# Prompt attention of a two-layer decoder: units ordered head by head, with three score banks and three accumulators

## The chip, the cores and the metric

The kernel runs on one core of one Trainium2 chip. The metric is the device time of one execution in microseconds, the median of several runs.

In this document PE is TensorE (its weight loads have a row of their own, PEld), DVE is VectorE, ACT is ScalarE, POOL is GpSimd and SP is SyncE. PSUM has eight banks, here called bank 0 to bank 7.

## What is computed

Two layers run for a prompt of 512 positions and for eight samples of eight positions each. Each layer has a joint input projection, three mixers (retention, sparse attention, gated delta rule), and an output projection. The part that matters here is the sparse attention of the prompt: 8 query heads in 2 key groups, head width 64, and three branches whose outputs are added with a gate for each head and branch:

```python
o_cmp, imp = _nsa_compressed(q, pos, k_c, v_c)                  # branch 0: 31 compressed keys
o_sel = ... _nsa_sel_attend(q_rot, ...)                         # branch 1: selected blocks
o_win = ... _window_attend(q_rot, ...)                          # branch 2: window of 512
no = gate[:, :, 0] * o_cmp + gate[:, :, 1] * o_sel + gate[:, :, 2] * o_win
no = no.reshape(B, T, NSA_WIDTH) * jax.nn.silu(pr['nsa_g'].astype(jnp.float32))
```

With a prompt of 512 positions all eight blocks are selected and the window reaches back to the start, so branches 1 and 2 are both plain causal attention over all keys up to the query, and branch 0 has 31 keys. Each branch is a masked softmax over its keys times its values.

## The kernel before

A layer is a series of stages with a barrier between them: input projection, retention, delta rule, prompt attention (`prompt_attention`), sample attention, output projection. Both layers go through the same code.

The second stage of `prompt_attention` is where the change lies. It works on 192 **units**; a unit is one tile of 128 queries (`qt`, 0 to 3), one branch (`br`, 0 to 2) and one head (`h`, 0 to 7). A unit of branch 0 has 31 keys, one of branch 1 or 2 has (qt + 1) * 128 keys. The order is the list `units`: for each query tile all heads of branch 0, then all of branch 1, then all of branch 2.

Every engine walks that list with its own lag, and semaphores tie them together. For a unit u:

1. PE, in its iteration u, makes the scores and adds the mask (`scores`, lines 1441 and 1443) in the bank `sbank(u)`.
2. DVE takes the row maximum (line 1501) and scales it (line 1503) (`biggest`).
3. ACT makes the exponentials with their sum (line 1486) into `Pr`.
4. PE, in its iteration u + 2, transposes them 128 keys at a time (`turn`, line 1452).
5. DVE for even u, ACT for odd u, copies them to `PT` (`copy`, line 1431).
6. PE, in its iteration u + 3, multiplies with the values (`values`, line 1464) into the head's 64 columns of an accumulator bank.
7. After the eighth head of a branch, DVE merges (`merge`, lines 1511 to 1521): it inverts the sums, multiplies the gates in, scales the 512 columns of the accumulator, adds them to `NO` and, for the last branch of the tile, multiplies by the output gate.

So PE's iteration v is: scores of v, transposes of v - 2, values of v - 3. DVE's iteration v is: maximum of v, copy of v - 2 if that is even, and the merge after unit v - 3 if v - 3 was the last of its group of heads. Within an engine everything is in order: while DVE merges, no maximum and no copy is made.

Before the change `DEEP` is 4 (four score banks and four buffers of `Pr`), and the accumulators are two banks used in turn by the 12 groups of eight units.

Of the kernel before, what the change touches and what calls it, by code (L numbers as in the profile page):

```python
# [17 lines left out]
ALU = mybir.AluOpType  # L18
# [8 lines left out]
HD = 64  # L27
H4 = 4
NH, G, R = 8, 2, 4
WIN = 512  # L30
P = 128
# [143 lines left out]
def b_(ap, axis, shape):  # L175

    return ap.unsqueeze(axis).broadcast_to(shape)
# [1125 lines left out]
def prompt_attention(nc, A, O, l, scope, sb, stage, v, U):  # L1303


    bk, cb, ident, MIX = v['bk'], v['cb'], v['ident'], v['MIX']
# [13 lines left out]
    with stage(["dve_s", "act_s", "pe_s", "rows", "kv"]) as (block, (dve_s, act_s, pe_s, rows, kv)):  # L1320
# [5 lines left out]
        @block.sync  # L1326
        def _(e):
            for i in range(2):
                e.dma_start(PG[:, i, :, :], O['kv_prompt'][l, 0].rearrange("(t p r) a g d -> t p r (a g d)", p=P, r=PAIRS)[i, :, :, 0:256]).then_inc(rows, 16)
            e.dma_start(QRP[:, :, :, :].rearrange("p t i c -> p t (i c)"), A['q_rot'].rearrange("(t p) c -> p t c", p=P)).then_inc(rows, 16)  # L1330
            e.dma_start(A['new_kv'].rearrange("b t c -> (b t) c"), v['US'][0:64, NKV:NKV + CW]).then_inc(kv, 16)
            first_pages(e, A, l, v, 0)
            e.wait_ge(kv, 16)
            for i in range(2):
                e.dma_start(new_values(v['US'])[:, :, i, :], A['new_kv'].rearrange("b t c -> t b c")[:, :, 256 * (i + 1) + P:256 * (i + 2)]).then_inc(kv, 16)
            e.wait_ge(kv, 48)
# [64 lines left out]
                    dve.done(e, f"T{'kl'[g]}{t}", nc.vector.tensor_copy(KT[g * HD:(g + 1) * HD, g, :, t * P:(t + 1) * P], bk(2, 4)[g * HD:(g + 1) * HD, 0:2, :]))  # L1401

    early.close()
    DEEP = 4
    sbank = lambda u: bk((0, 1, 6, 7)[u % DEEP])
    Pr = sb(scope, "Pr", [P, DEEP, SEQ])
    PT = sb(scope, "PT", [P, 2, 4, P])
    mx = sb(scope, "mx", [P, DEEP, 2])
    SUM = sb(scope, "SUM", [P, 2, NH])
    fac = sb(scope, "fac", [P, NH])  # L1410
    T1 = sb(scope, "T1", [P, 512])
    NO = sb(scope, "NO", [P, 512])
    units = [(qt, br, h) for qt in range(4) for br in range(3) for h in range(NH)]
    NU = len(units)
    with stage(["score", "shift", "exped", "turned", "copied_dve", "copied_act", "used", "link_s", "merged"]) as \
            (block, (score, shift, exped, turned, copied_dve, copied_act, used, link_s, merged)):
        copied = [copied_dve, copied_act]

        def keys(u):
            qt, br, h = units[u]  # L1420
            return NCP if br == 0 else (qt + 1) * P

        def copy(e, u):

            n = keys(u)
            m, k = (n, 1) if n < P else (P, n // P)
            e.wait_ge(turned, u + 1)
            if u >= 2:
                e.wait_ge(used, u - 1)
            o, i = PT[0:m, u % 2, 0:k, :], bk(2 + u % 2, 4)[0:m, 0:k, :]  # L1430
            (nc.scalar.activation(o, i, ACT.Copy) if u % 2 else nc.vector.tensor_copy(o, i)).then_inc(copied[u % 2], 1)

        @block.tensor
        def _(e):
            def scores(u):
                qt, br, h = units[u]
                g, r, n = h // R, h % R, keys(u)
                if u >= DEEP:
                    e.wait_ge(exped, u - DEEP + 1)
                kt = KCG[:, g, 0:n] if br == 0 else KT[:, g, br - 1, 0:n]  # L1440
                nc.tensor.matmul(sbank(u)[:, 0:n], QT[:, min(br, 1), r, qt * P:(qt + 1) * P], kt, start=True, stop=False)  # L1441
                m = cb('cmask', 32)[:, qt, 0:n] if br == 0 else cb('causal')
                nc.tensor.matmul(sbank(u)[:, 0 if br == 0 else qt * P:n], cb('identb'), m, start=False, stop=True).then_inc(score, 1)  # L1443

            def turn(u):
                n = keys(u)
                e.wait_ge(exped, u + 1)
                if u >= 2:
                    e.wait_ge(copied[u % 2], u // 2)
                for j in range(-(-n // P)):  # L1450
                    m = min(P, n - j * P)
                    mm = nc.tensor.transpose(bk(2 + u % 2, 4)[0:m, j, :], Pr[:, u % DEEP, j * P:j * P + m], ident)  # L1452
                mm.then_inc(turned, 1)

            def values(u):
                qt, br, h = units[u]
                g, n, q = h // R, keys(u), u // NH
                e.wait_ge(copied[u % 2], u // 2 + 1)
                if h == 0 and q >= 2:
                    e.wait_ge(merged, q - 1)  # L1460
                for j in range(-(-n // P)):
                    m = min(P, n - j * P)
                    vv = VC[0:m, 0, g * HD:(g + 1) * HD] if br == 0 else U[j][:, NKV + P + 256 * br + g * HD:NKV + P + 256 * br + (g + 1) * HD]
                    mm = nc.tensor.matmul(bk(4 + q % 2)[:, h * HD:(h + 1) * HD], PT[0:m, u % 2, j, :], vv, start=(j == 0), stop=(j == -(-n // P) - 1))
                mm.then_inc(used, 1)

            for u in range(NU + 3):
                if u < NU:
                    scores(u)
                if 2 <= u < NU + 2:  # L1470
                    turn(u - 2)
                if u >= 3:
                    values(u - 3)

        @block.scalar
        def _(e):
            for u in range(NU + 2):
                if u >= 2 and u % 2:
                    copy(e, u - 2)
                if u < NU:  # L1480
                    qt, br, h = units[u]
                    n = keys(u)
                    e.wait_ge(shift, u + 1)
                    if u >= DEEP:
                        e.wait_ge(turned, u - DEEP + 1)
                    nc.scalar.activation(Pr[:, u % DEEP, 0:n], sbank(u)[:, 0:n], ACT.Exp, scale=SCALE, bias=mx[:, u % DEEP, 1:2],  # L1486
                                         accum_out=SUM[:, (u // NH) % 2, h:h + 1]).then_inc(exped, 1)

        @block.vector
        def _(e):  # L1490
            links = [0]

            def link(ins):
                links[0] += 1
                ins.then_inc(link_s, 1)
                e.wait_ge(link_s, links[0])

            def biggest(u):
                n = keys(u)
                e.wait_ge(score, u + 1)  # L1500
                link(nc.vector.tensor_reduce(mx[:, u % DEEP, 0:1], sbank(u)[:, 0:n], AX.X, ALU.max))  # L1501

                nc.vector.tensor_scalar(mx[:, u % DEEP, 1:2], mx[:, u % DEEP, 0:1], -1e20, -SCALE, ALU.max, ALU.mult).then_inc(shift, 1)  # L1503

            def merge(u):
                qt, br, h = units[u]
                q = u // NH
                hb = lambda ap: ap.rearrange("p (h c) -> p h c", c=HD)
                e.wait_ge(used, u + 1)
                e.wait_ge(exped, u + 1)  # L1510
                link(nc.vector.tensor_scalar(fac[:, :], SUM[:, q % 2, :], 1e-30, None, ALU.max))
                link(nc.vector.reciprocal(fac[:, :], fac[:, :]))
                link(nc.vector.tensor_tensor(fac[:, :], fac[:, :], U[qt][:, NGATE + br * NH:NGATE + (br + 1) * NH], ALU.mult))
                dst = NO if br == 0 else T1
                links[0] += 1
                nc.vector.tensor_tensor(hb(dst[:, :]), hb(bk(4 + q % 2)), b_(fac[:, :], 2, [P, NH, HD]), ALU.mult).then_inc(link_s, 1)
                e.wait_ge(link_s, links[0])
                if br:
                    link(nc.vector.tensor_tensor(NO[:, :], NO[:, :], T1[:, :], ALU.add))
                if br == 2:  # L1520
                    link(nc.vector.tensor_tensor(MIX[:, qt, 256:768], NO[:, :], U[qt][:, NG:NG + 512], ALU.mult))
                nc.vector.engine_nop().then_inc(merged, 1)

            for u in range(NU + 3):
                if u < NU:
                    biggest(u)
                if 2 <= u < NU + 2 and u % 2 == 0:
                    copy(e, u - 2)
                if u >= 3 and (u - 3) % NH == NH - 1:
                    merge(u - 3)  # L1530


# [641 lines left out]
```

## Time and profile before

| | |
|---|---|
| three runs | 2633.17, 2610.85, 2634.86 us; median 2633.17 |
| the profiled execution | 2642.13 us, its span 2640.5 us |
| busy over the span | PE 84%, PE's weight loads 63%, DVE 50%, ACT 28%, POOL 11% |
| mean granted clock of TensorE | 0.854 of full |

The span is the time from the first to the last instruction. "Granted clock" is what the throttle let TensorE have: 1.00 is 2.4 GHz, 0.50 is 1.2 GHz. A busy PE says only that some matmul was in flight, not that it ran at the full clock.

### The profile page before, as it was taken

The numbers are of one execution on the slowest core, as the hardware profiler recorded it, in microseconds if no ns is written. First come the engines' busy times: TensorE is split into PE (matmuls) and PEld (weight loads), VectorE is DVE, ScalarE is ACT, GpSimd is POOL, SyncE is SP. The second block draws the span as 40 slices with busy tenths as digits, with TensorE's granted clock in tenths as the row PEclk, the third lists the DMA queues.
The fourth block names the chain that finished last, engine by engine and source line by source line (L and its number), as shares of the span: only waits on it lengthen the run. The fifth ranks groups of instructions, "written<-read, shape, count | busy, mean of one in ns | idle before, by whom it ended". The sixth has DMA issues, their size and how long they took to land. (4 is left out here: it accounts for less than half of the span.)

```text
span 2640.5 us, 35927 instructions
## 1 busy us (share of the span) xinstructions
PE 2229.7 (84%) x12280; PEld 1657.8 (63%) x12280; DVE 1321.1 (50%) x3088; ACT 730.7 (28%) x1512; POOL 302.4 (11%) x516
## 2 busy tenths in 40 slices
PE   6989748738999999997889896586499999999977
PEld 3644448737767888886354444486376678888863
DVE  1252566534654666654213434765355556666532
ACT  2120002103434454440212101111044445444302
POOL 0000000000013433420000000000000234334100
PEclk9999769756879999996989997687567889999859
DMA  4443010020027886851035330100300368868420
GB/s 148 147 151 113 26 35 1 1 79 7 1 52 168 192 188 152 181 124 72 2 113 168 137 109 10 35 1 2 84 1 1 89 150 191 179 152 190 107 72 36
DMA packets 175947, 242.04 MB, mean 92 GB/s; under 512 B 50118, under 2 KB 132838, under 8 KB 175084
## 3 DMA queue, kind: packets, MB, share of 16 engines
q1 hardware_dynamic: 151180, 172.51, 24.5%
q0 software_dynamic: 24576, 67.14, 10.8%
q8 instruction: 100, 1.64, 0.3%
q14 instruction: 91, 0.75, 0.1%
HBM read 223.17 MB, written 24.97 MB: 94 GB/s over the span
## 5 line engine op out<-in xcount | busy, mean ns | idle before, releaser
L601 PE MATMUL bank<-W,hT 128*128 128x512 f32 (+3 forms) x1152 | 449.0, 544 | 30.6 <-DMA W<-in_w_in 21.5
L1282 POOL DMA_DIRECT2D SHARED<-in_cache_nsa_kv x256 | 151.5, 592 | 2048.7 <-issue 734.4
L601 PEld LDWEIGHTS bank<-W,hT 128*128 128x128 f32 x1152 | 219.0, 195 | 230.8 <-issue 184.5
L1225 PE MATMUL bank<-XT,W 128*128 128x256 f32 (+1 forms) x768 | 250.8, 462 | 0.0
L1214 ACT ACTIVATE XT<-bank 128x512 f32<-128x512 f32 x256 | 140.3, 593 | 132.6 <-PE bank L1207 132.5
L1282 POOL DMA_DIRECT2D PS<-in_cache_nsa_kv x256 | 150.7, 589 | 140.6 <-issue 128.2
L1225 PEld LDWEIGHTS bank<-XT,W 128*128 128x128 f32 x768 | 134.9, 190 | 49.7 <-issue 36.9
L1207 PE MATMUL bank<-CF,RP 128*128 128x128 f32 x1024 | 146.9, 290 | 7.6 <-DVE RP L1195 6.9
L1708 PE MATMUL bank<-QBD,PS 128*128 128x64 f32 x1024 | 141.9, 287 | 0.0
L1501 DVE TENSOR_REDUCE mx<-bank 128x1 f32<-128x31 f32 (+4 forms) x192 | 74.6, 389 | 132.5 <-PE bank L1443 131.1
L1708 PEld LDWEIGHTS bank<-QBD,PS 128*128 128x128 f32 x1024 | 139.7, 210 | 0.7
L1688 PEld LDWEIGHTS bank<-PB,PS 128*128 128x128 f32 x1024 | 132.7, 209 | 10.6 <-issue 6.7
L1688 PE MATMUL bank<-PB,PS 128*128 128x64 f32 x1024 | 135.1, 292 | 3.5 <-ACT PB L1854 3.5
L1207 PEld LDWEIGHTS bank<-CF,RP 128*128 128x128 f32 x1024 | 120.3, 151 | 18.9 <-DVE RP L1195 10.6
L1441 PE MATMUL bank<-KT,QT 128*128 128x128 f32 (+3 forms) x256 | 125.5, 580 | 0.0
L366 DVE COPY UP<-bank 128x512 f32<-128x512 f32 (+3 forms) x36 | 21.4, 604 | 199.9 <-PE bank L601 199.7
L2092 PE MATMUL bank<-Wo,mT 128*128 128x512 f32 x256 | 114.6, 611 | 5.9 <-DMA Wo<-in_w_out 5.9
L1486 ACT ACTIVATE Pr<-bank,mx 128x31 f32<-128x31 f32 (+4 forms) x192 | 85.6, 446 | 120.1 <-DVE mx L1503 119.1
L1195 DVE COPY RP<-SHARED 128x512 f32<-128x512 f32 x256 | 98.6, 426 | 24.9 <-DMA SHARED<-in_cache_nsa_kv 12.8
L368 ACT ACTIVATE UP<-bank 128x512 f32<-128x512 f32 (+3 forms) x36 | 18.7, 527 | 302.9 <-PE bank L601 302.8
L1452 PE MATMUL bank<-CF,Pr 128*128 128x128 f32 (+1 forms) x384 | 88.9, 317 | 14.8 <-ACT Pr L1486 14.8
L1858 ACT ACTIVATE PS<-bank 128x512 f32<-128x512 f32 x128 | 75.8, 593 | 89.2 <-PE bank L1695 88.3
(378 smaller groups left out, 3699.4 us busy)
## 6 DMA issues: line engine op xcount, KB each, us to landing
SHARED<-in_cache_nsa_kv SPq DMA_DIRECT2D x256, 128.0 KB, 6.1
SHARED<-in_cache_nsa_kv POOLq DMA_DIRECT2D x256, 128.0 KB, 5.3
PS<-in_cache_nsa_kv SPq DMA_DIRECT2D x256, 128.0 KB, 6.1
PS<-in_cache_nsa_kv POOLq DMA_DIRECT2D x256, 128.0 KB, 5.7
W<-in_w_in SPq DMA_DIRECT2D x48, 512.0 KB, 4.5
XS<-scratch_conv_p SPq DMA_DIRECT2D x24, 384.0 KB
PW<-in_state_nsa_win SPq DMA_DIRECT2D x16, 512.0 KB, 3.8
Wo<-in_w_out SPq DMA_DIRECT2D x4, 2048.0 KB, 11.8
```

The source lines that it names most:

```text
L601: return nc.tensor.matmul(bk((c * NTILE + t) % 8)[:, 0:b - a], hT[:, k, t * P:(t + 1) * P], W[:, k // 2, k % 2, 0:b - a], start=(k == 0), ...
L1195: dve.done(e, self.name("R", i), nc_(self.v).vector.tensor_copy(self.RP[:, i % self.RING, :, :, :].rearrange("p h r d -> p r h d"), self.P ...
L1207: mm = nc_(self.v).tensor.transpose(self.v['bk'](6 + i % 2, 4)[:, h, :], self.RP[:, i % self.RING, h, :, :].rearrange("p r d -> p (r d)"), ...
L1214: act.done(e, self.name("X", i), nc_(self.v).scalar.activation(self.columns()[:, :, :, i, :], self.v['bk'](6 + i % 2).rearrange("p (h s n) ...
L1225: mm = nc_(self.v).tensor.matmul(out, self.v['W1'][:, kv, s, :], seg[:, s], start=(s == 0), stop=(s == SEG // PAIRS - 1))
L1282: e.dma_start(where[side * HD:(side + 1) * HD, slot, :, :], A['cache_nsa_kv'][l, page].rearrange("(p r) a g d -> p r (a g d)", r=PAIRS)[:, ...
L1441: nc.tensor.matmul(sbank(u)[:, 0:n], QT[:, min(br, 1), r, qt * P:(qt + 1) * P], kt, start=True, stop=False)
L1452: mm = nc.tensor.transpose(bk(2 + u % 2, 4)[0:m, j, :], Pr[:, u % DEEP, j * P:j * P + m], ident)
L1486: nc.scalar.activation(Pr[:, u % DEEP, 0:n], sbank(u)[:, 0:n], ACT.Exp, scale=SCALE, bias=mx[:, u % DEEP, 1:2], accum_out=SUM[:, (u // NH) ...
L1688: mm = nc.tensor.matmul(bk(bank)[:, 256:320], vs[i], PB[:, o + i, :], start=(i == 0), stop=(i == len(vs) - 1))
L1708: mm = nc.tensor.matmul(out[:, i % 8, :], PSg[:, i, 0:P], QBD[:, 1, b, :], start=(i % 8 == 0), stop=False, skip_group_check=True)
L2092: mm = nc.tensor.matmul(bk(4 - 4 * h + t), mT[:, k, t * P:(t + 1) * P], W[:, k, h * 512:(h + 1) * 512], start=(k == 0), stop=(k == KD - 1))
```

## The change

`units` is reordered: within a query tile the outer loop is now over heads, and each head goes through branch 1, branch 2 and branch 0. Because the three branches of a tile are then all open at the same time, each has an accumulator bank of its own (4, 5 and 7), and the sums have a place for each branch. The third bank is taken from the scores, so `DEEP` goes from 4 to 3. A branch is complete only with the eighth head, so its merge comes after unit 21, 22 or 23 of the 24 of a tile, in three consecutive iterations of DVE. The number and the size of all operations stay as they were; `NO` is now begun by branch 1 and finished by branch 0.

```diff
-    DEEP = 4
-    sbank = lambda u: bk((0, 1, 6, 7)[u % DEEP])
+    DEEP = 3
+    BRANCHES = (1, 2, 0)
+    OUT = {1: 4, 2: 5, 0: 7}
+    sbank = lambda u: bk((0, 1, 6)[u % DEEP])
...
-    SUM = sb(scope, "SUM", [P, 2, NH])
+    SUM = sb(scope, "SUM", [P, 2, 3, NH])
...
-    units = [(qt, br, h) for qt in range(4) for br in range(3) for h in range(NH)]
+    FIRST, LAST = BRANCHES[0], BRANCHES[-1]
+    units = [(qt, br, h) for qt in range(4) for h in range(NH) for br in BRANCHES]
...
-                if h == 0 and q >= 2:
-                    e.wait_ge(merged, q - 1)
+                if h == 0 and qt:
+                    e.wait_ge(merged, 3 * (qt - 1) + BRANCHES.index(br) + 1)
...
-                    mm = nc.tensor.matmul(bk(4 + q % 2)[:, h * HD:(h + 1) * HD], PT[0:m, u % 2, j, :], vv, start=(j == 0), stop=(j == -(-n // P) - 1))
+                    mm = nc.tensor.matmul(bk(OUT[br])[:, h * HD:(h + 1) * HD], PT[0:m, u % 2, j, :], vv, start=(j == 0), stop=(j == -(-n // P) - 1))
...
-                dst = NO if br == 0 else T1
+                dst = NO if br == FIRST else T1
...
-                if br:
+                if br != FIRST:
                     link(nc.vector.tensor_tensor(NO[:, :], NO[:, :], T1[:, :], ALU.add))
-                if br == 2:
+                if br == LAST:
                     link(nc.vector.tensor_tensor(MIX[:, qt, 256:768], NO[:, :], U[qt][:, NG:NG + 512], ALU.mult))
...
-                if u >= 3 and (u - 3) % NH == NH - 1:
+                if u >= 3 and units[u - 3][2] == NH - 1:
                     merge(u - 3)
```

## Rows read from the trace of the kernel before

**Rows 1.** Busy us of each engine in the first layer's stage, then the granted clock.

```profile
610.00:775.00 165.00, 154.57 (x864) 118.51 (x864) 89.56 (x300) 67.97 (x241) 0.00 (x0) 0.77 0.00 1
```

**Rows 2.** The same view of that stage, three stretches cut where the clock changes.

```profile
612.90:629.80 16.90, 16.90 (x75) 13.62 (x74) 7.51 (x35) 6.33 (x31) 0.00 (x0) 0.50 0.00 0
...
636.80:660.30 23.50, 22.88 (x96) 17.90 (x94) 11.84 (x48) 8.13 (x38) 0.00 (x0) 0.50 0.00 1
...
725.50:742.30 16.80, 16.80 (x49) 10.00 (x50) 6.29 (x19) 4.90 (x17) 0.00 (x0) 0.50 0.00 0
```

**Rows 3.** Timeline of PE at the full clock: start us, duration us, instruction, idle before.

```profile
675.36 0.36 PE L1441 MATMUL bank<-KCG,QT 128*128 128x31 f32 x2
675.55 0.18 PE L1443 MATMUL bank<-CB 128*128 128x31 bf16 x1
...
677.75 0.41 PE L1441 MATMUL bank<-KCG,QT 128*128 128x31 f32 x2
678.00 0.18 PE L1443 MATMUL bank<-CB 128*128 128x31 bf16 x1
...
678.23 0.43 PE L1464 MATMUL bank<-VCp,PT 31*128 31x64 f32 x2
...
678.59 0.41 PE L1441 MATMUL bank<-KCG,QT 128*128 128x31 f32 x2
...
762.55 1.08 PE L1441 MATMUL bank<-KT,QT 128*128 128x512 f32 x2
...
763.52 0.61 PE L1452 MATMUL bank<-CF,Pr 128*128 128x128 f32 x4
...
763.96 1.00 PE L1464 MATMUL bank<-UP,PT 128*128 128x64 f32 x8
...
764.80 1.08 PE L1441 MATMUL bank<-KT,QT 128*128 128x512 f32 x2
```

**Rows 4.** The same timeline where PE waits, with idle time and its releaser in brackets.

```profile
636.11 0.33 PE L1452 MATMUL bank<-CF,Pr 128*128 128x128 f32 x1 [1.59 <-ACT Pr L1486]
...
645.69 0.42 PE L1452 MATMUL bank<-CF,Pr 128*31 128x128 f32 x1 [0.62 <-ACT Pr L1486]
...
671.40 0.44 PE L1452 MATMUL bank<-CF,Pr 128*128 128x128 f32 x2 [0.79 <-ACT Pr L1486]
...
680.84 0.30 PE L1452 MATMUL bank<-CF,Pr 128*31 128x128 f32 x1 [1.82 <-ACT Pr L1486]
```

**Rows 5.** Timeline of DVE in the last merge of the third query tile.

```profile
721.07 0.17 DVE L1511 TENSOR_SCALAR fac<-SUM 128x8 f32<-128x8 f32 x1 [0.16 <-PE bank L1464]
...
721.71 0.69 DVE L1516 TENSOR_TENSOR T<-bank,fac 128x512 f32<-128x512 f32 x1
...
722.44 0.69 DVE L1519 TENSOR_TENSOR NO<-NO,T 128x512 f32<-128x512 f32 x1
...
723.16 0.69 DVE L1521 TENSOR_TENSOR MIX<-NO,UP 128x512 f32<-128x512 f32 x1
723.90 0.18 DVE L1501 TENSOR_REDUCE mx<-bank 128x1 f32<-128x31 f32 x1
```

**Rows 6.** Timeline of DVE and ACT on units of 512 keys.

```profile
761.47 0.69 DVE L1501 TENSOR_REDUCE mx<-bank 128x1 f32<-128x512 f32 x1
...
762.19 0.15 DVE L1503 TENSOR_SCALAR mx<-mx 128x1 f32<-128x1 f32 x1
762.27 0.69 DVE L1431 COPY PT<-bank 128x512 f32<-128x512 f32 x1
762.38 0.69 ACT L1486 ACTIVATE Pr<-bank,mx 128x512 f32<-128x512 f32 x1 [0.23 <-DVE mx L1503]
...
762.97 0.19 ACT L1486 ACTIVATION_READ_ACCUMULATOR Pr<-bank,mx 128x1 f32 x1
```

**Rows 7.** Timeline of DVE and PE at the end of the stage.

```profile
773.03 0.17 DVE L1511 TENSOR_SCALAR fac<-SUM 128x8 f32<-128x8 f32 x1 [2.38 <-PE bank L1464]
...
777.06 0.66 PE L1738 MATMUL bank<-CF,QRS 64*128 64x64 f32 x4 [4.07 <-PEq L200]
```

More of the change, by code:

```diff
@@ L1456, in values @@
                 qt, br, h = units[u]
-                g, n, q = h // R, keys(u), u // NH
+                g, n = h // R, keys(u)
                 e.wait_ge(copied[u % 2], u // 2 + 1)
-                if h == 0 and q >= 2:
-                    e.wait_ge(merged, q - 1)
+                if h == 0 and qt:
+                    e.wait_ge(merged, 3 * (qt - 1) + BRANCHES.index(br) + 1)
                 for j in range(-(-n // P)):
@@ L1486, in _ @@
                     nc.scalar.activation(Pr[:, u % DEEP, 0:n], sbank(u)[:, 0:n], ACT.Exp, scale=SCALE, bias=mx[:, u % DEEP, 1:2],
-                                         accum_out=SUM[:, (u // NH) % 2, h:h + 1]).then_inc(exped, 1)
+                                         accum_out=SUM[:, qt % 2, br, h:h + 1]).then_inc(exped, 1)
         @block.vector
@@ L1506, in merge @@
                 qt, br, h = units[u]
-                q = u // NH
                 hb = lambda ap: ap.rearrange("p (h c) -> p h c", c=HD)
@@ L1510, in merge @@
                 e.wait_ge(exped, u + 1)
-                link(nc.vector.tensor_scalar(fac[:, :], SUM[:, q % 2, :], 1e-30, None, ALU.max))
+                link(nc.vector.tensor_scalar(fac[:, :], SUM[:, qt % 2, br, :], 1e-30, None, ALU.max))
                 link(nc.vector.reciprocal(fac[:, :], fac[:, :]))
                 link(nc.vector.tensor_tensor(fac[:, :], fac[:, :], U[qt][:, NGATE + br * NH:NGATE + (br + 1) * NH], ALU.mult))
-                dst = NO if br == 0 else T1
+                dst = NO if br == FIRST else T1
                 links[0] += 1
-                nc.vector.tensor_tensor(hb(dst[:, :]), hb(bk(4 + q % 2)), b_(fac[:, :], 2, [P, NH, HD]), ALU.mult).then_inc(link_s, 1)
+                nc.vector.tensor_tensor(hb(dst[:, :]), hb(bk(OUT[br])), b_(fac[:, :], 2, [P, NH, HD]), ALU.mult).then_inc(link_s, 1)
                 e.wait_ge(link_s, links[0])
-                if br:
+                if br != FIRST:
                     link(nc.vector.tensor_tensor(NO[:, :], NO[:, :], T1[:, :], ALU.add))
-                if br == 2:
+                if br == LAST:
                     link(nc.vector.tensor_tensor(MIX[:, qt, 256:768], NO[:, :], U[qt][:, NG:NG + 512], ALU.mult))
```

## The prediction

> **What bounds the kernel now.** I read first the busy time of the first layer's stage [rows 1]: PE is busy 154.6 of 165 us, DVE 89.6, ACT 68.0, and the granted clock is only 0.77. So PE is the bound, but for a large part of the stage it runs at half of its clock. The second layer does the same. Next I cut the stage where the clock changes [rows 2]. Four stretches run at 0.50 (1.2 GHz): one of 16.9 us that the stage starts with, one of 23.5 us, one of 16.7 us that lies between the last two shown, and one of 16.8 us, 73.9 us in all. The reader should see that PE is busy all through three of them, so each costs half its length whatever lies in it. Then I asked the timeline where PE waits [rows 4]. There are five waits, each behind a merge on DVE: 1.59, 0.62, 0.79, 1.82 and once more 1.82 us, 6.6 us together. The three long ones (1.59, 1.82, 1.82) each stand right before a fall of the clock; the 0.79 us one doesn't. The 0.62 us one lies inside the long half-clock stretch, and that stretch is the one that lasts 23.5 us instead of 17. So the stage has three kinds of cost: PE's own work, the waits behind merges, and the half clock that follows them.
>
> **PE's own work.** No operation is added or removed; what can change is how neighbours overlap. A unit of 31 keys (a short unit) costs from start to start 0.84 us at full clock, one of 512 keys 2.25 us [rows 3]. Score and mask of a short unit take 0.19 us when values of a long unit precede them and 0.25 us when values of a short one do [rows 3]. The scores of v follow the values of v - 4 on PE. In the new order v - 4 is of branch 2 when v is short, so always long; before, v - 4 is short itself from a tile's fifth head on, and throughout the first tile: 16 + 4 = 20 units. That makes 20 x 0.05 = 1.0 us less in a layer. The rest of the chain of a short unit (transposes, values) is as long as before by the same rows. PE's work is thus equal but for **-1.0 us**. That is the first finding against a large gain: a short unit between long ones has nothing to hide behind, since it waits for nothing where PE is the bound.
>
> **Fewer score banks.** PE now waits, before the scores of v, for the exponentials of v - 3 rather than v - 4. But in its iteration v - 1 it has already done the transposes of v - 3, which need the same exponentials. ACT's wait for a free buffer of `Pr` is the transposes of v - 3, which come before the scores of v on PE. Both are met when they are reached: **0 us**. The same holds for the wait on the accumulators: values of unit 24 wait for the merge of branch 1, but PE's iteration 27 transposes unit 25 first, whose maximum lies behind that merge on DVE.
>
> **The merges.** A merge is 0.64 us of small steps, 0.73 us of scaling, 0.72 us of adding and 0.74 us for the output gate [rows 5]: 1.36 us for the first branch, 2.09 for the second, 2.83 for the last. The same 12 merges remain, but they now come in four packs of three, three of them between tiles and one at the end. I follow the pack between the third and the fourth tile, at full clock, from the moment t when DVE starts the maximum of unit 72 (512 keys). DVE: maximum and scaling 0.80 (0.72 to the scaling, 0.08 more until it can go on) [rows 6]; copy of unit 70, 384 keys, 0.56 (read between 0.69 for 512 and 0.28 for a short one); merge 1.36; maximum of 73 0.80; merge 2.09; maximum of 74, a short one, 0.30; copy of 72 0.69; 0.05 until PE sees it. Sum 6.65. Queued behind the merges are these maxima and the copy; PE needs the copy for the values of 72. PE meanwhile, with 0.11 us a transpose chunk, 0.21 us a value chunk and 0.97 us for scores and mask of 512 keys [rows 3]: transposes and values of 70 and 69 0.94; iteration 73 0.97 + 0.11 + 0.61; iteration 74 0.22 + 0.53 + 0.36; iteration 75 scores and transposes 0.97 + 0.44. Sum 5.15, begun 0.2 before t. PE waits 6.65 - 4.95 = **1.7 us**. The same sum for 384 keys (DVE 6.1, PE 3.8) gives 2.3 us between second and third tile, and for 256 keys (DVE 5.6, PE 2.7) 2.9 us between first and second. After that wait comes the last merge of the pack: 2.83 + 0.72 + 0.19 to ACT + 0.83 for exponentials and their sum [rows 6] = 4.6 us until the transposes of 75, against PE's work of 3.0 us at full clock and 5.9 at half. If the clock has fallen, this second wait is gone there; between second and third tile it is 4.3 against 4.5, also gone, and between first and second 4.1 against 3.3, so 0.8 us remains. Waits in all: 2.9 + 0.8 + 2.3 + 1.7 = 7.7 against 6.6 now: **+1.1 us** a layer. What goes are the waits in mid tile (1.59 and 0.79); what takes their place are longer ones at the tile's end.
>
> **The end of the stage.** Now only one merge is left when PE is done: 773.03 to 775.8, 2.8 us, and the next stage's PE starts at 777.06 [rows 7]. In the new order DVE begins the first of the last pack about 1.3 us before PE ends and needs 1.36 + 2.09 + 2.83 = 6.3 us: 5.0 us behind PE. **+2.2 us** a layer. Nothing covers it, for the barrier waits for DVE.
>
> **The half clock.** The first stretch begins with the stage and stays. Each pack holds a wait of at least 1.7 us, and the clock fell after every wait from 1.59 up [rows 4], so I expect three more stretches. The first has a wait of 0.8 us inside it, like the one of 23.5 us now; the other two have none. So 17 + 23.5 + 17 + 17 again, half of it lost, **0 us**. The Trainium skill, "TensorE: Matmul & The Clock Gate", section "HAM oscillation", says that idle gaps of PE within a loop bring back the half rate each time, and that the loop should be ordered so that PE stays busy. The trace agrees as to the gaps; whether the new order closes them is the point of the first rival.
>
> **Sum.** -1.0 + 1.1 + 2.2 = +2.3 us a layer, +4.6 us for two. The profiled execution took 2642.1 us (span 2640.5), so 2646.7 on its scale. That execution was 9.0 us above the median of 2633.2; on the median's scale I predict 2637.8, rounded to 2638. The three runs spread over 24 us, so below about 1% (26 us) a measurement of this kernel can't tell a difference from none.
>
> **Rivals.** (1) *The clock stays up.* For: around the third pack PE runs dense long matmuls, and 1.7 us is close to the 1.59 and not above it by much; 0.79 us did no harm. Against: a second wait of 1.5 us would follow the first within 5 us. If the third pack doesn't pull the clock down, 16.8 / 2 - 1.5 = 6.9 us are saved in a layer, 13.8 in both: 2624. If the second doesn't either (16.7 / 2 - 1.9 = 6.5), 2611; if none does (23.5 / 2 - 1.6 = 10.2), 2591. (2) *Longer half-clock stretches*, the case on the slow side: a wait inside a stretch stretched it from 17 to 23.5 us. Between second and third tile my margin is 0.2 us (4.3 against 4.5), between third and fourth 1.3 us. If a wait does fall inside both, 3.4 us x 2 x 2 = 13 us are added: 2651. It decides from the point where the last merge and the exponentials behind it outlast PE's work at half clock. (3) *Switching between matrix shapes.* Before, a short unit's transposes and its values (31 rows) follow each other; now they lie in different iterations among matrices of 128 rows, one switch more for each of 64 short units. The two value matmuls of 31 rows cost 0.36 us against 0.21 for two of a long unit [rows 3], so I bound a switch by 0 and 0.15 us: up to 9.6 us, 2647. I take zero, since where transposes of a short unit now precede long values the trace has no pause. The Trainium skill, "TensorEngine Tiling (Array Packing)", section "Key Properties", has it that changing the tiling mode drains TensorE; by that the bound's upper end would hold. (4) *The score banks bind after all*: they can't by the order above unless a semaphore's passage counts; I give it no time.
>
> **Chances.** The forecast 0.62; the clock stays up 0.18 (third pack alone 0.10, two 0.05, all 0.03); longer stretches 0.12; switches 0.08. The range takes in two packs without a fall (2611) and longer stretches together with part of the switches (2657). Faster by over 1% needs all three falls gone, or two and a lucky median: 0.09. Slower by over 1% needs two of the slow cases at once, or something that I don't see: 0.10. Within 1%: 0.81.
>
> **What the profile would show.** PE's instructions and busy time unchanged at equal clock. No wait on PE behind a merge in mid tile; three pairs of waits at the tiles' ends, for the transposes behind a maximum and for the values behind DVE's copy, the latter 1.7 to 1.9 us. The clock at 0.50 four times in the stage, about 74 us together. From PE's last matmul of the stage to the end of the last merge 5 us in place of 2.8. The stage 2 us longer. I am wrong if the clock's stretches are fewer or longer, or if a short unit costs more than 0.84 us among long ones.

## The result, and the profile after

The changed kernel takes 2618.03 us (median of 19 runs, 2598.47 to 2644.45) against 2635.98 us (median of 19 runs, 2609.84 to 2649.97) for the one before, run beside it: a ratio of 0.9932 with a 95% interval of 0.9902 to 0.9961. It is some 18 us faster. The forecast was 4.6 us slower, so the sign was wrong, though 2618 lies within the stated range. The profiled execution took 2606.3 us, 35.8 us less than the one before; most of that is not the change's, as shown below.

The page's span, PE's totals, and the granted clock by fortieths of the span:

```profile
span 2604.7 us, 35927 instructions
...
PE 2180.4 (84%) x12280; PEld 1622.3 (62%) x12280; DVE 1321.7 (51%) x3088; ACT 727.3 (28%) x1512; POOL 302.9 (12%) x516
...
PEclk9999868855899999996979997697559999999979
```

To compare the stage itself, this section and the next measure it from PE's first score matmul to the end of the last multiplication by the output gate. Before it was 164.9 and 165.2 us in the two layers; now it is 157.3 in both, so the two stages give 15.5 us. The medians differ by 18 us, by 10 to 26 with the interval, so the stages can be all of the gain. The other 20.3 us between the two profiled executions lie in code that is the same in both kernels (2310.4 and 2290.1 us outside the two stages), and that part varies by itself: in e1 and e9 below, which are one kernel, it is 2291.9 and 2314.9 us. (The stage has 96 units in each layer; 192 is the number for both.) The same views as before, first the busy time of each engine (stretch, its us, busy us with instructions of PE, PEld, DVE, ACT and POOL, then the granted clock), cut where the clock changes; the last row is of the second layer:

```profile
610.00:775.00 165.00, 149.53 (x890) 117.93 (x890) 95.98 (x313) 69.11 (x245) 2.35 (x4) 0.82 0.02 7
613.80:661.30 47.50, 46.74 (x200) 38.77 (x201) 22.65 (x92) 18.10 (x78) 0.00 (x0) 0.50 0.00 1
661.30:688.90 27.60, 24.16 (x170) 18.96 (x169) 18.61 (x66) 13.14 (x50) 0.00 (x0) 0.99 0.00 1
688.90:692.20 3.30, 3.30 (x15) 2.51 (x13) 1.28 (x4) 0.67 (x2) 0.00 (x0) 0.50 0.00 0
692.20:763.50 71.30, 68.70 (x471) 52.11 (x469) 42.29 (x122) 32.61 (x104) 0.00 (x0) 1.00 0.01 1
...
2019.90:2023.30 3.40, 3.40 (x12) 2.06 (x11) 0.92 (x3) 0.83 (x4) 0.00 (x0) 0.51 0.00 0
```

The clock over these 165 us went from 0.77 [rows 1] to 0.82, with the first microseconds of the next stage in it now. At 0.50 there is now one stretch of 47.5 us, all of the first tile and a part of the second, and one of 3.3 us; the second layer has 47.7 us and 3.4 us. That is 50.8 us against the 73.9 us of four stretches before [rows 2], 23 us less. Neither the one long stretch nor the short ones look like the 17 us pieces that I had counted with. In the row of 47.5 us PE is busy 46.7 us: it is not for want of work that the clock stays down.

PE's waits behind merges, in the timeline:

```profile
646.79 1.12 PE L1467 MATMUL bank<-UP,PT 128*128 128x64 f32 x4 [0.23 <-DVE PT L1434]
...
650.87 0.69 PE L1455 MATMUL bank<-CF,Pr 128*128 128x128 f32 x2 [0.54 <-ACT Pr L1489]
...
682.81 0.88 PE L1467 MATMUL bank<-UP,PT 128*128 128x64 f32 x6 [1.64 <-DVE PT L1434]
...
686.99 0.55 PE L1455 MATMUL bank<-CF,Pr 128*128 128x128 f32 x3 [1.61 <-ACT Pr L1489]
...
722.97 1.10 PE L1467 MATMUL bank<-UP,PT 128*128 128x64 f32 x8 [1.38 <-DVE PT L1434]
...
727.38 0.66 PE L1455 MATMUL bank<-CF,Pr 128*128 128x128 f32 x4 [1.18 <-ACT Pr L1489]
```

Together with one of 0.20 they make 6.8 us, against 6.6 before [rows 4]: the two waits that I worked out at 1.7 and 1.5 us for the third pack came out at 1.38 and 1.18, those of the second pack at 1.64 and 1.61 (forecast: 2.3 in the first, none in the second, since I had the clock at half there). After the third pack's two waits the clock did not fall in the first layer; after the second pack's it didn't fall in the second layer.

A whole cycle of three units (384, 384 and 31 keys) at full clock:

```profile
702.32 0.91 PE L1444 MATMUL bank<-KT,QT 128*128 128x384 f32 x2
703.07 0.22 PE L1446 MATMUL bank<-CB 128*128 128x128 bf16 x1
...
706.59 0.91 PE L1444 MATMUL bank<-KT,QT 128*128 128x384 f32 x2
```

702.32 to 706.59 is 4.27 us; before, two units of 1.71 and a short one of 0.84 made 4.26. And the end of the stage, DVE and then PE of the next stage:

```profile
762.09 0.17 DVE L1513 TENSOR_SCALAR fac<-SUM 128x8 f32<-128x8 f32 x1 [0.15 <-PE bank L1467]
...
767.81 0.69 DVE L1523 TENSOR_TENSOR MIX<-NO,UP 128x512 f32<-128x512 f32 x1
```

```profile
769.75 1.08 PE L1740 MATMUL bank<-CF,QRS 64*128 64x64 f32 x8 [6.30 <-PEq L200]
```

Between PE's last matmul and its next it now idles 6.30 us, 4.07 before [rows 7].

### The profile page after: what moved, and what is told of

It reads as the page before. It is cut to its first block and busy times, and to the rows that moved or that the text cites. A ratio compares the mean times of both kernels' runs of the same rounds, so it can differ in the third digit from the quotient of the medians.

```text
span 2604.7 us, 35927 instructions
## 1 busy us (share of the span) xinstructions
PE 2180.4 (84%) x12280; PEld 1622.3 (62%) x12280; DVE 1321.7 (51%) x3088; ACT 727.3 (28%) x1512; POOL 302.9 (12%) x516
## 3 DMA queue, kind: packets, MB, share of 16 engines
q8 instruction: 100, 1.64, 0.3%
## 5 line engine op out<-in xcount | busy, mean ns | idle before, releaser
L1710 PE MATMUL bank<-QBD,PS 128*128 128x64 f32 x1024 | 133.6, 275 | 0.0
L1710 PEld LDWEIGHTS bank<-QBD,PS 128*128 128x128 f32 x1024 | 131.1, 199 | 0.7
L1444 PE MATMUL bank<-KT,QT 128*128 128x128 f32 (+3 forms) x256 | 117.5, 549 | 3.7 <-PEq L200 3.7
L1467 PE MATMUL bank<-UP,PT 128*128 128x64 f32 x640 | 97.9, 289 | 6.5 <-DVE PT L1434 6.5
L1467 PEld LDWEIGHTS bank<-UP,PT 128*128 128x128 f32 x640 | 94.9, 217 | 8.7 <-DVE PT L1434 8.6
```

The source lines that it names most:

```text
L1467: mm = nc.tensor.matmul(bk(OUT[br])[:, h * HD:(h + 1) * HD], PT[0:m, u % 2, j, :], vv, start=(j == 0), stop=(j == -(-n // P) - 1))
L1710: mm = nc.tensor.matmul(out[:, i % 8, :], PSg[:, i, 0:P], QBD[:, 1, b, :], start=(i % 8 == 0), stop=False, skip_group_check=True)
```

## The experiments

Three theories are named in the expectations. **A**: runs of 31-key units hold a fallen clock down, waits bring it down. **B**, the prediction's: each fall comes from a wait and lasts about 17 us, whatever is computed. **C**: the 31-key units bring the clock down by themselves. All the results in one table first (stage in us for both layers, or where it says units, to the end of PE's last matmul of them, which before is 162.1 and 162.4; us at half clock in PE's part of the stage, read in steps of half a microsecond; sum of PE's waits over 0.15 us behind its first score matmul, first layer):

| kernel | stage | at half clock | waits |
|---|---|---|---|
| before | 164.9, 165.2 | 75.5, 75.0 | 7.4 |
| changed | 157.3, 157.3 | 51.5, 51.5 | 7.5 |
| e1 order by branch, compressed last | 156.2, 150.6 | 60, 43 | 5.0 |
| e2 before, merges at the end | units 144.9, 147.9 | 51, 58 | 0.8 |
| e3 before, short units in 128-row form | 141.4, 139.9 | 37.0, 34.5 | 9.8 |
| e4 changed, tile 0 by branch | 150.4, 152.7 | 30.5, 41.0 | 8.4 |
| e5 before with the new banks | 164.9, 165.3 | 74.5, 75.5 | 7.4 |
| e6 changed, 128-row form | 137.3, 144.5 | 17.0, 41.0 | 9.3 |
| e7 by branch, 128-row form | 137.7, 140.5 | 19, 30 | 10.3 |
| e10 as e7, timed | 137.5, 140.1 | 19, 26 | 10.3 |
| e8 before, only values in 128-row form | 141.6, 141.2 | 38.0, 38.5 | 9.6 |
| e9 as e1, timed | 154.9, 155.0 | 54, 53 | 5.9 |
| e11 e10 with merges taken apart | 131.8, 134.3 | 10, 16 | 7.7 |
| e12 changed, merges at the end | units 136.5, 139.6 | 34, 41 | 0.7 |

**Do the banks cost anything?** Only the three score banks and three accumulators, in the old order:

```diff
-    BRANCHES = (1, 2, 0)
+    BRANCHES = (0, 1, 2)
-    units = [(qt, br, h) for qt in range(4) for h in range(NH) for br in BRANCHES]
+    units = [(qt, br, h) for qt in range(4) for br in BRANCHES for h in range(NH)]
```

> The order of the kernel before (compressed, selected, window, branch by branch) with the three score banks and three accumulators of the changed one. If the banks cost nothing: the waits of the kernel before at the same places (1.59, 0.62, 0.79, 1.82, 1.82 us), half-clock stretches of 17, 24, 17 and 17 us, stage 163 to 167 us. If they cost, a unit of 256 keys has a period above 1.17 us at full clock.

The stretches at half clock and, from the timeline, the first long wait:

```profile
616.80:633.80 17.00, 17.00 (x74) 13.65 (x74) 7.52 (x35) 6.44 (x32) 0.00 (x0) 0.50 0.01 1
640.80:664.30 23.50, 22.88 (x95) 17.90 (x95) 12.02 (x48) 8.19 (x38) 0.00 (x0) 0.50 0.00 1
```

```profile
639.94 0.33 PE L1455 MATMUL bank<-CF,Pr 128*128 128x128 f32 x1 [1.59 <-ACT Pr L1489]
```

The stages are 164.9 and 165.3 us, the waits and the stretches those of the kernel before. The banks cost nothing; the order alone makes the difference.

**Do waits bring the clock down?** The kernel before, every merge after the last unit (PE then writes over accumulators that are not merged yet, so this kernel serves for its times alone):

```diff
-                if u >= 3 and (u - 3) % NH == NH - 1:
-                    merge(u - 3)
+            e.wait_ge(used, NU)
+            e.wait_ge(exped, NU)
+            for u in range(NH - 1, NU, NH):
+                merge(u)
...
-                if h == 0 and q >= 2:
-                    e.wait_ge(merged, q - 1)
```

> The kernel before with all twelve merges moved behind the last unit, so that no maximum waits behind a merge; the attention output is then made of later contents of the accumulators, all operations are still done. If only waits of PE bring the clock down (theories A and B alike), the clock rises once at 17 us and stays at 1.00 to the end of the units: PE's units end 131 to 137 us after the start (162 before). If runs of 31-key units bring it down without a wait (theory C), there are still stretches at 0.50 in tiles 1 to 3 and the units end after 145 us or more.

Busy time in stretches cut at the clock's changes:

```profile
641.30:655.30 14.00, 14.00 (x51) 9.98 (x52) 4.21 (x19) 4.63 (x20) 0.00 (x0) 0.51 0.01 2
655.30:675.80 20.50, 20.50 (x163) 17.69 (x162) 12.71 (x50) 13.16 (x50) 0.00 (x0) 1.00 0.00 1
675.80:685.80 10.00, 10.00 (x31) 6.14 (x29) 3.53 (x10) 3.09 (x9) 0.00 (x0) 0.50 0.00 0
...
713.30:723.30 10.00, 10.00 (x26) 4.88 (x25) 3.01 (x9) 2.55 (x10) 0.00 (x0) 0.50 0.00 0
```

and PE's timeline at the second fall:

```profile
674.27 0.41 PE L1441 MATMUL bank<-KCG,QT 128*128 128x31 f32 x2
674.52 0.18 PE L1443 MATMUL bank<-CB 128*128 128x31 bf16 x1
674.54 0.28 PE L1452 MATMUL bank<-CF,Pr 128*31 128x128 f32 x1
674.75 0.43 PE L1462 MATMUL bank<-VCp,PT 31*128 31x64 f32 x2
675.11 1.14 PE L1441 MATMUL bank<-KT,QT 128*128 128x384 f32 x2
676.04 0.31 PE L1443 MATMUL bank<-CB 128*128 128x128 bf16 x1
```

PE is busy 20.50 of 20.50 us, then 10.00 of 10.00, with no wait that the profile shows (it models the ends of matmuls, so pauses inside overlapping ones would not appear), and the clock still goes from 1.00 to 0.50 between them. The timeline shows where: the matmul of 384 keys at 675.11 takes 1.14 us where 0.91 is its time after short units, the mask behind it 0.31 in place of 0.22. It comes at the end of eight short units in a row. A fall comes in every tile after the first, once six to eight scores of its run of short units have begun, in one case one score later, and the clock returns among the long units. This is theory C, though the first layer's units ended 0.1 us under its bound of 145 us; A and B both had the clock at 1.00 here. In tiles 1 to 3 the waits are not needed for the fall. In tiles 2 and 3 they make little difference to its place (with them it comes after the sixth or seventh short score has begun) and more to its length: 17 us with the waits, 10 to 14 us without. In tile 0 it is otherwise: the fall behind the wait of 1.59 us, among 128-key units [rows 4], is missing here, so that one did need its wait. Waits and runs of short units each bring the clock down.

The same edit on the changed kernel:

> The changed kernel with all twelve merges behind the last unit, so that no unit waits for a merge (the attention output is made of later contents of the accumulators). If the 47 us at half clock of tile 0 come from its units (every third has the 31-row form), the first stretch still lasts over 35 us, and there is no other. If they came from the waits of the first pack, it ends before 25 us.

```profile
615.40:649.40 34.00, 34.00 (x154) 28.89 (x153) 13.17 (x61) 13.87 (x62) 0.00 (x0) 0.50 0.00 0
649.40:748.60 99.20, 99.20 (x697) 77.09 (x695) 54.18 (x171) 49.89 (x171) 0.00 (x0) 1.00 0.01 1
```

Without any merge among the units, the changed order runs all of tile 0 at half clock (34.0 us here, 1 short of my bound, and 41 in the second layer), and then never falls again. So most of the long stretch of the changed kernel comes from its units, every third of which is short among 128-key ones; the 7 to 14 us more that it lasts there go with the merges' waits. In the other tiles the long units outweigh the short ones. The two short stretches of the changed kernel are gone with the waits. That is what the change does: short units spread among units of 256 to 512 keys no longer pull the clock down, and those among units of 128 keys do so more than before.

**What in a short unit does it?** The 31-key units, in the order of the kernel before, transpose all 128 columns of their exponentials (what an earlier unit left there in columns 31 to 127) and multiply with a value tile whose rows 31 to 127 are zero; the output stays as it was. The value tile and the exponentials' buffers are set to zero first, and the copies take all 128 rows:

```diff
-                    m = min(P, n - j * P)
+                    m = P
                     mm = nc.tensor.transpose(bk(2 + u % 2, 4)[0:m, j, :], ...
...
-                    m = min(P, n - j * P)
+                    m = P
                     vv = VC[0:m, 0, g * HD:(g + 1) * HD] if br == 0 else ...
```

> The kernel before, order untouched, but the 31-key units transpose and multiply all 128 columns and rows of their buffers (the 97 extra value rows are zero): the same number of PE instructions with the shape of a 128-key unit. Theory A in the form that the 31-row shapes hold the clock down: the half-clock stretches after the long waits shrink from 17 us to under 8, stage 140 to 152 us. Theory B: stretches stay at 17 us; the short unit falls from 0.84 to about 0.62 us at full and from 1.45 to about 1.0 at half clock, stage 150 to 156 us.

```profile
627.40:644.40 17.00, 15.72 (x81) 14.37 (x81) 9.12 (x39) 6.84 (x33) 0.00 (x0) 0.50 0.00 1
668.40:671.40 3.00, 3.00 (x12) 2.21 (x13) 1.03 (x5) 0.83 (x5) 0.00 (x0) 0.50 0.00 0
702.40:709.40 7.00, 6.28 (x23) 4.41 (x24) 2.90 (x15) 2.72 (x14) 0.00 (x0) 0.52 0.00 0
```

Stages of 141.4 and 139.9 us: 24 us less in each layer by a change of form alone, three times what the change of order gave. The third and fourth stretch, 17 us each before, now last 3 and 7 us; the first lasts 10 in place of 17, the second 17 in place of 23.5. The next kernel does it for the values alone and leaves the transposes at 31 columns:

> The kernel before with only the values of the 31-key units made over 128 rows (zero rows of values added); their transposes keep 31 columns. The values take 0.18 in place of 0.36 us and the pause between transpose and values goes, so a short unit has about 0.6 us at full clock. If the values in 31-row form are what keeps the clock down, half-clock time falls to the 35 us of the kernel with both in 128-row form and the stage to 140 to 145 us; if the transposes with 31 columns are, it stays at 60 us or more and the stage at 150 us or more.

Its timeline of one short unit at full clock, its weight loads (PEld) for the values, and, behind the same in the kernel before, one of its stretches at half clock:

```profile
665.90 0.36 PE L1442 MATMUL bank<-KCG,QT 128*128 128x31 f32 x2
666.10 0.18 PE L1444 MATMUL bank<-CB 128*128 128x31 bf16 x1
666.13 0.28 PE L1453 MATMUL bank<-CF,Pr 128*31 128x128 f32 x1
666.24 0.37 PE L1465 MATMUL bank<-VCp,PT 128*128 128x64 f32 x2
666.45 0.36 PE L1442 MATMUL bank<-KCG,QT 128*128 128x31 f32 x2
```

```profile
666.18 0.30 PEld L1465 LDWEIGHTS bank<-VCp,PT 128*128 128x128 f32 x2
```

and in the kernel before, with the load ahead of it:

```profile
678.00 0.11 PEld L1452 LDWEIGHTS bank<-CF,Pr 128*31 128x31 f32 x1
678.23 0.29 PEld L1464 LDWEIGHTS bank<-VCp,PT 31*128 31x128 f32 x2
```

```profile
669.00:676.00 7.00, 6.81 (x28) 5.23 (x29) 2.83 (x13) 2.81 (x15) 0.00 (x0) 0.51 0.00 0
```

From 665.90 to 666.45 a short unit takes 0.55 us where it took 0.84 [rows 3]: from the mask to the values it is 0.14 in place of 0.23, the values take 0.21 in place of 0.36, and the scores 0.20 in place of 0.25. Part of it is plain in the weight loads: with 128 rows the load for the values starts 0.06 us ahead of its matmul (666.18, 666.24), under matmuls in flight; with 31 rows it starts only with its matmul (both at 678.23), 0.23 us behind the load before it. From 32 short units a layer this comes to 9 us at full clock, an estimate; the rest of the 24 us is the clock's, less 2 us of longer waits. Half-clock time is 38.0 and 38.5 us, as with both forms changed, and the stage 141.6 and 141.2. So it is the values with 31 rows, not the transposes with 31 columns. What it is about them that brings the clock down these runs don't separate: it may be the rows of the array that stand idle, the late weight loads, or that a run of eight short units now lasts 4.4 us in place of 6.7. The Trainium skill, "TensorEngine Tiling (Array Packing)", section "Key Properties", says that changing the tiling mode drains TensorE; the rows agree with a cost of that kind, 0.29 us in each short unit at full clock, though no run shows whether 31 rows are another mode. It was paid before the change as well as after.

**Does the order by head matter?** The changed kernel by branch, compressed branch last:

> The changed kernel with only the order put back to branch by branch (selected, window, compressed); three score banks and three accumulators stay. Stage lengths are from PE's first matmul to the last merge: 165 us before, 157 us changed. If the banks cost nothing and the order does everything, and if the clock's return is held up by runs of 31-key units (theory A), the stage starts with 128-key units alone and the first half-clock stretch is under 12 us, while the runs of 31-key units at a tile's end still hold it down: 60 to 75 us at half clock in all, stage 158 to 166 us. If every stretch lasts 17 us from its wait on whatever is computed (theory B, that of the prediction), the first stretch is 17 us and the stage 163 to 166. If three score banks cost time, the unit's period at full clock is over 1.17 us for 256 keys.

and the same again, timed:

> The order by branch with the compressed branch last, banks as in the changed kernel, now timed. Its stage took 156.2 and 150.6 us in the two layers against 157.3 in the changed kernel and 165 before. If that difference is real, it is 21 to 27 us faster than before (ratio 0.990 to 0.992), so at least as fast as the head by head order at 0.9932, and the gain of the change needs no order by head.

```profile
610.80:614.30 3.50, 3.50 (x20) 3.23 (x20) 1.83 (x8) 1.87 (x9) 0.00 (x0) 0.53 0.00 0
628.30:641.80 13.50, 13.50 (x47) 9.54 (x47) 6.30 (x22) 3.79 (x16) 0.00 (x0) 0.50 0.00 1
```

```profile
628.04 0.42 PE L1455 MATMUL bank<-CF,Pr 128*31 128x128 f32 x1 [1.17 <-ACT Pr L1489]
```

The timed ratio is 0.9932 with an interval of 0.9900 to 0.9963, the very ratio of the order by head, and a smaller gain (17 us) than the 21 to 27 us that I expected from e1's stages. My bound of 158 to 166 us for its stage was too high: 150.6 to 156.2 in four layers seen. Here the clock does fall in or just behind the runs of short units, with a wait of 1.17 us or 1.09 in each, but the first tile's 128-key units come first and mostly at full clock, the waits are shorter, and behind the merge of 2.83 us, which now falls under the next tile's long units, PE doesn't wait at all. The last fall, in tile 3's short units, lasts 20 us, 14 of them beyond PE's part of the stage, which the stage's length leaves out and the timed ratio holds. Two orders with different stretches reach the same time: nothing in the gain is owed to going head by head as such.

Tile 0 by branch and the others by head should join the good halves of both:

> The changed kernel with tile 0 branch by branch (selected, window, compressed) and tiles 1 to 3 head by head. Theory A: the first half-clock stretch, 47 us in the changed kernel, ends within 12 us of the stage's start since tile 0 begins with 16 units of 128 keys; a second begins at the merges of tile 0 and lasts under 20 us; stage 145 to 153 us against 157. Theory B: a stretch of 17 us at the start, one of 17 to 24 after tile 0: 153 to 157 us.

```profile
617.30:633.80 16.50, 14.72 (x118) 12.31 (x118) 11.69 (x56) 10.98 (x48) 0.00 (x0) 1.00 0.00 1
633.80:660.80 27.00, 26.11 (x101) 19.87 (x100) 12.04 (x45) 8.75 (x37) 0.00 (x0) 0.50 0.01 1
```

16.5 us at full clock from the start in the first layer, in place of a stretch at half clock; 150.4 and 152.7 us, within what theory A, and C with it, gave. The stretch that begins at tile 0's merges was to last under 20 us, and lasts 27.0, in the second layer 20.5. In the second layer the start has 6.5 us at half clock and the second pack 10.5. Its whole time, seen once (2618.49 us beside 2618.67 for the kernel before), doesn't show this, since single runs scatter by more than the 27 us that two stages would give (the 19 runs of the kernel before span 40 us).

**The 128-row form in the new orders**, by head and by branch:

> The changed kernel with 31-key units that transpose and multiply all 128 columns and rows. Theory C (31-key units in the 31-row form bring the clock down and keep it down): the 47 us stretch of tile 0 ends within 20 us of the stage's start; with about 0.3 us less in each of 32 short units the stage falls from 157 to 132 to 142 us. If the 31-row form has no part in the clock, the first stretch stays at 40 us or more and the stage is 146 to 150 us.

```profile
608.20:611.20 3.00, 3.00 (x18) 2.87 (x18) 1.47 (x7) 1.54 (x8) 0.00 (x0) 0.50 0.00 0
631.70:638.70 7.00, 5.85 (x27) 4.98 (x27) 4.41 (x13) 2.38 (x9) 0.00 (x0) 0.52 0.00 1
1884.50:1912.00 27.50, 27.50 (x146) 25.86 (x145) 13.73 (x64) 12.99 (x60) 0.00 (x0) 0.50 0.00 1
```

> Selected, window, compressed, branch by branch, with the 128-row form of the short units: the order of the first experiment. If the order by head gives something of its own, this is slower than the changed kernel with the 128-row form. If the gain of the change is only that short units don't stand in runs, it is as fast or faster, since one merge at a time makes shorter waits: 132 to 141 us.

By head the first stretch shrank from 47 us to 3 in the first layer but to 27.5 in the second (the last row), so the stage is 137.3 and 144.5 us, and what I expected (20 us at most, stage up to 142) held in the first layer only. Tile 0 alone, with units of at most 128 keys, still holds the clock down at times when nothing else differs, and why it did in one layer and not in the other stays open. By branch it is 137.7 and 140.5, within what I expected, and its stretches among the units are 7 us at most; one more begins 2 us before the last of PE's matmuls and goes on beyond them. Timed:

> By branch with the 128-row form of the short units, timed: stages of 137.7 and 140.5 us against 165 should give 52 us, ratio 0.979 to 0.982.

```profile
697.60:704.60 7.00, 6.12 (x23) 4.38 (x24) 3.03 (x16) 2.56 (x13) 0.00 (x0) 0.51 0.01 2
```

2580.44 us (6 runs) against 2631.88 (17 runs), ratio 0.9803, interval 0.9761 to 0.9844, as its stages let expect. Last, in the same kernel, the merge taken apart, so that maxima and copies go on between its parts:

```diff
-                if br != FIRST:
-                    link(nc.vector.tensor_tensor(NO[:, :], NO[:, :], T1[:, :], ALU.add))
-                if br == LAST:
-                    link(nc.vector.tensor_tensor(MIX[:, qt, 256:768], ...
-                nc.vector.engine_nop().then_inc(merged, 1)
+                nc.vector.engine_nop().then_inc(merged, 1)
+                if br != FIRST:
+                    later.append(lambda: link(nc.vector.tensor_tensor(NO[:, :], NO[:, :], T1[:, :], ALU.add)))
+                if br == LAST:
+                    later.append(lambda: link(nc.vector.tensor_tensor(MIX[:, qt, 256:768], ...
...
+                if later:
+                    later.pop(0)()
...
+            for step in later:
+                step()
```

> The same with the merge taken apart: only the part that reads the accumulator (1.36 us) stays in one piece, the addition and the output gate are done one each in the following iterations of DVE. Six of the waits of 0.8 to 1.6 us a layer should fall to under 0.9, and with no wait that long the clock should stay up after tile 0: stage 128 to 134 us, 62 to 72 us faster than before. If waits don't matter to the clock once the 31-row form is gone, only their own 5 us a layer are saved: 132 to 136 us.

```profile
627.30:630.80 3.50, 3.50 (x15) 2.74 (x15) 1.26 (x6) 1.28 (x7) 0.00 (x0) 0.53 0.00 0
654.80:658.30 3.50, 3.50 (x19) 2.71 (x17) 0.95 (x6) 1.15 (x7) 0.00 (x0) 0.51 0.02 5
```

2571.67 us (6 runs), ratio 0.977, interval 0.9724 to 0.9816: 60 us less than before (62 to 72 expected) and the best of all, though its interval overlaps that of the kernel without the last step. The longest wait fell from 1.61 to 0.88 us, with one of 0.49 close behind it. The clock still fell for 3 to 7 us around the tiles' ends, so my "no fall after tile 0" was wrong; half-clock time in PE's part of the stage is 10 and 16 us. Its last fall comes 3.5 us before the end of PE's units and lasts 17 us, most of it in the next stage.

## Why the prediction was wrong

**The half clock** is the step that failed: the term put at 0 us came to about -10 us a layer. Its two sentences were "each costs half its length whatever lies in it" and the count "17 + 23.5 + 17 + 17 again", from waits that had each been followed by a fall. Six waits out of six in two layers had a fall behind them, but four of the six stood in a run of short units: e2 has those four falls, and they come without the waits, while the changed kernel has waits of up to 1.6 us without a fall. The length of a stretch is no constant of 17 us but depends on what PE computes in it: 47.5 and 3.3 us in the changed kernel, 34 us in tile 0 without any wait (e12), 7 us where 17 stood once the short units' values have 128 rows (e8). I had the evidence in the trace and didn't line it up: in the kernel before the clock came back 4 to 7 us after the last values of the short units in every tile. What the change gave here is 23 us less at half clock in a layer (24 in the table's steps).

What those 23 us are worth is a second error in the same step. From the stage's difference of -7.6 us, with +0.2 for waits, 0 for PE's own work and +2.2 for the end, the clock must have given about 10 us, not 11.6. Half clock nearly doubles the time of long matmuls (the scores of 384 keys went from 0.70 to 1.38 us, start to start), but a short unit goes only from 0.84 to 1.45 us, a loss of 42% of a stretch full of them.

**PE's own work**: -1.0 forecast, 0 measured (4.27 against 4.26 us a cycle). The 0.05 us that a short unit's scores save after long values is lost again by the long unit's scores after short values (0.75 in place of 0.70 us). I had looked at one of the two neighbours. The count was off too: the first four units of the stage have no values before them, so it is 16 and not 20 units.

**Fewer score banks**: 0 forecast, 0 shown by e5. **The merges**: waits of 7.7 us forecast, 6.8 found; the places were right, the sum partly by luck. The first pack's waits came to 0.77 us and not 3.7, because PE was at half clock there, and the second pack's second wait of 1.61 us came where I had none, because PE was at full clock. **The end of the stage**: +2.2 us forecast, 6.30 - 4.07 = +2.2 measured.

**The rivals**: the first, "the clock stays up", came nearest: the 2618 lie between its 2624 for one pack without a fall and its 2611 for two. Its price was wrong, though: it took a fall that did come to last 17 us at half clock, and those that came among long units lasted 3.3 and 3.4 us. Nor did it see that tile 0 would stay at half clock. Longer stretches (the second rival) did come, but in tile 0 and from its units. Switching between shapes costs nothing additional here: the cycle of 4.27 us holds one more switch than before. The Trainium skill's section "HAM oscillation" in "TensorE: Matmul & The Clock Gate" names idle gaps as the cause of the half rate; the trace agrees that falls follow gaps closely, but e2 shows a fall where the profile has no gap at all, and here the measurement decides.

## What to carry to other kernels

Where a busy engine runs at a reduced clock, don't take the wait in front of the fall for its cause: move the waits away in one run, and keep the work. Matmuls with few rows can cost more than the same matmuls padded with zeros to 128 rows, as here, both for themselves (0.36 against 0.21 us for two) and through the clock of everything around them (75 against 38 us at half clock). And a reordering should be compared with the plainest other order before its gain is given to the idea behind it.

## What the runs showed of the hardware

With no idle time on PE in the profile, runs of eight units of 31-key attention, each with two float32 matmuls of 31 rows, took the granted clock from 1.00 (2.4 GHz) to 0.50 (1.2 GHz) in every tile after the first (e2); with those matmuls on 128 rows, half-clock time in the stage fell from 75 to 38 us (e8). A fall amid long matmuls lasted 3.3 and 3.4 us in the changed kernel, and once 10.5 us (e4, second layer); one in or before a run of short units lasted 10 to 24 us in orders by branch; the one at the start of the changed kernel's stage lasted 47.5 us, with PE busy for 46.7. Weight loads of 31-row matmuls started with their matmul, those of 128-row matmuls 0.06 us ahead of it.
